# A gated mixer block with a 32-expert layer: the experts' weights fetched as 1 MB pieces into sixteen places instead of 2 MB pieces into eight

## The reference, cut to what matters

```python
h2 = rmsnorm(x, ffn_norm_g)                       # 256 tokens x 1024
logits = h2 @ router_w + router_b                 # 32 experts, the best 4 of each token are used
for e in range(32):
    g = jnp.minimum(t @ w_gate[e] + b_gate[e], 7.0)
    u = jnp.clip(t @ w_up[e] + b_up[e], -7.0, 7.0)
    act = (u + 1.0) * (g * jax.nn.sigmoid(1.702 * g))
    out = out + comb[:, e:e + 1] * (act @ w_down[e] + b_down[e])
```

## Time and profile before

| | before |
|---|---|
| device time, median of 3 runs | 1172.27 us (1169.89 to 1173.79) |
| span of the profiled execution | 1169.7 us |
| PE busy | 1102.9 us (94%) |
| DVE, ACT, POOL busy | 281.6, 190.4, 62.6 us |
| bytes read from HBM | 431.21 MB |
| mean rate over the span | 370 GB/s |
| experts' transfers | 192 of 2048 KB |

### The profile page before, as it was taken

The page is one execution under the profiler, slowest core; times in us unless marked ns, Lnnn a source line. Parts: engine busy times, 40 slices in busy tenths (PEclk is TensorE's granted clock), DMA queues, the critical chain, the costliest instruction groups (busy, mean ns, idle before and its releaser), DMA issues.

```text
span 1169.7 us, 13269 instructions
## 1 busy us (share of the span) xinstructions
PE 1102.9 (94%) x5385; PEld 463.3 (40%) x5385; DVE 281.6 (24%) x632; ACT 190.4 (16%) x361; POOL 62.6 (5%) x58
## 2 busy tenths in 40 slices
PE   6998998999999999999999999999999999999998
PEld 3787995333333333333333333333333333333332
DVE  4978664111111111111111111111111111111112
ACT  3645632100110010001000100001000100010000
POOL 0194120000000000000000000000000000000000
PEclk9989998999999999999999999999999999999999
DMA  8612478799999999999999999999999999999996
GB/s 314 256 73 108 171 295 334 293 402 409 409 409 409 410 409 409 409 410 410 409 409 410 410 409 410 409 410 410 409 409 410 410 410 409 410 410 409 409 409 259
DMA packets 116942, 432.55 MB, mean 370 GB/s; under 512 B 5557, under 2 KB 6106, under 8 KB 116922
## 3 DMA queue, kind: packets, MB, share of 16 engines
q1 hardware_dynamic: 116634, 431.60, 93.3%
q10 hardware_dynamic: 288, 0.67, 0.2%
HBM read 431.21 MB, written 1.05 MB: 370 GB/s over the span
## 4 chain that ended last, share of the span: by engine, by line
PE 48%; DMA 41%; DVE 7%; ACT 2%; SPq 1%; issue 1%; DVEq 0%; ACTq 0%
DMA ring<-in_exp_w_up 41%; PE ps L752 27%; PE ps L711 5%; PE ps L759 3%; PE ps L717 3%; PE ps L724 2%; PE ps L490 2%; PE ps L492 2%; PE ps L491 2%; DVE ring_r L1071 1%; DMA ring<-in_w_in 1%; SPq L434 1%; ACT ring_r L812 1%; DVE arena L1140 1%; DVE arena L1126 1%; PE ps L777 1%
## 5 line engine op out<-in xcount | busy, mean ns | idle before, releaser
L752 PE MATMUL ps<-ring,arena 128*64 128x512 f32 x3072 | 685.9, 594 | 32.5 <-DMA ring<-in_exp_w_gate 28.0
L752 PEld LDWEIGHTS ps<-ring,arena 128*64 128x64 f32 x3072 | 218.9, 137 | 486.8 <-issue 414.5
L1315 DVE TENSOR_SCALAR arena<-ps 128x512 f32<-128x512 f32 x32 | 22.1, 692 | 507.6 <-PE ps L752 507.6
L759 PE MATMUL ps<-arena 128*64 128x512 f32 x384 | 102.9, 614 | 0.3 <-issue 0.3
L1325 DVE TENSOR_SCALAR arena<-ps 128x512 f32<-128x512 f32 x32 | 22.1, 692 | 244.4 <-PE ps L752 244.4
L969 ACT COPY arena<-ps 128x512 f32<-128x512 f32 x32 | 18.8, 587 | 333.9 <-PE ps L711 333.9
L724 PE MATMUL ps<-arena 64*128 64x512 f32 x264 | 65.6, 615 | 0.8 <-ACT arena L975 0.8
L967 ACT ACTIVATE arena<-arena 128x512 f32<-128x512 f32 x32 | 20.1, 630 | 280.7 <-DVE arena L1315 280.7
L490 PE MATMUL ps<-ring_r 128*128 128x256 f32 (+1 forms) x192 | 61.1, 318 | 4.2 <-DVE ring_r L1071 2.4
L711 PE MATMUL ps<-arena 128*64 128x512 f32 x264 | 64.0, 607 | 0.8 <-DVE arena L1261 0.8
L975 ACT COPY arena<-ps 128x512 f32<-128x512 f32 x32 | 18.8, 586 | 249.0 <-PE ps L752 249.0
(11 more groups left out here) (185 smaller groups left out, 637.6 us busy)
## 6 DMA issues: line engine op xcount, KB each, us to landing
ring<-in_exp_w_gate SPq DMA_DIRECT2D x64, 2048.0 KB, 23.5
ring<-in_exp_w_up SPq DMA_DIRECT2D x64, 2048.0 KB, 23.7
ring<-in_exp_w_down SPq DMA_DIRECT2D x64, 2048.0 KB, 23.7
ring<-in_w_in SPq DMA_DIRECT2D x8, 2048.0 KB, 9.4
ring<-in_w_out SPq DMA_DIRECT2D x2, 2048.0 KB, 7.8
xt<-in_x SPq DMA_DIRECT2D x4, 512.0 KB, 6.9
ring<-in_pool_up SPq DMA_DIRECT2D x1, 2048.0 KB, 7.9
ring<-in_attn_up SPq DMA_DIRECT2D x1, 2048.0 KB, 8.6
```

What stands on the lines that cost most here:

```text
L752: last = mm(ps[BLOCK * half:BLOCK * (half + 1), bank, :], src[:, c, k % 2, :], slot(n)[:, c, HALF * half:HALF * (half + 1)], start=False, ...
L759: mm(ps[BLOCK * half:BLOCK * (half + 1), bank, :], this_e[:, buf, k, :], bias_rows[:, HALF * half:HALF * (half + 1)], start=True, stop=False)
L1315: v.tensor_scalar(g1, ps[:, 4, :], LIMIT, None, ALU.min).then_inc(g_ready, 1)
```

## The change: 1 MB pieces, sixteen places, one run of 8 KB per partition

Each place is halved (`PART_W`), which makes sixteen (`RING`), and an expert's weights are twelve pieces, four for each matrix (`PARTS_OF_W`). The rows are dealt to the partitions in another way: row `512 * h + 4 * p + 2 * d + c` goes to partition p. So the two rows of a piece that go to one partition are neighbours in HBM, and lie in it and in SBUF as one run of 8 KB; the next partition's run begins 16 KB further, and the other half of each 16 KB is the next piece.

The products must meet the features in the same order. Where a feature is placed is decided when DVE writes `h2` and `act_out`: both are now written through a permuted pattern (chunk-major in memory, read in the natural order), so that each 32-bit result goes 512 bytes behind the one before. The gains of the norm, which came from a turned tile `cols`, are now loaded in that order by one small transfer of their own on ACT's queue. The number of matrix products and their sizes stay as they are. The front's pieces get semaphores of their own (`front_in`).

```diff
-PIECES_PER_EXPERT = 6
+PIECES_PER_EXPERT = 12
+PARTS_OF_W = PIECES_PER_EXPERT // 3
+RING = 16
+PART_W = PIECE // 2
...
-                        w = A[name][0].rearrange("e (c p) n -> p e c n", p=P)
-                        for half in range(2):
-                            n = PIECES_PER_EXPERT * j + 2 * m + half
-                            if first and n < SLOTS:
-                                front_piece_free(sp, LEFT_BY[n])
+                        w = A[name][0].rearrange("e (h p d c) n -> p e h d (c n)", h=2, p=P, d=2)
+                        for part_w in range(PARTS_OF_W):
+                            n = PIECES_PER_EXPERT * j + PARTS_OF_W * m + part_w
+                            if first and n < RING:
+                                front_piece_free(sp, LEFT_BY[n // 2])
                             else:
...
-                                sp.wait_ge(piece_done, at * (UNROLL * PIECES_PER_EXPERT) + (n - SLOTS + 1))
-                            src = w[:, bass.ds(step * UNROLL + j, 1), 4 * half:4 * half + 4, :]
-                            src = src.rearrange("p e c n -> p (e c) n")
-                            sp.dma_start(slot(n), src).then_inc(slot_in[ORDER[n % SLOTS]], 16)
+                                sp.wait_ge(piece_done, at * (UNROLL * PIECES_PER_EXPERT) + (n - RING + 1))
+                            half, pair_of = divmod(part_w, 2)
+                            src = w[:, bass.ds(step * UNROLL + j, 1), half:half + 1, pair_of:pair_of + 1, :]
+                            src = src.rearrange("p e h d n -> p (e h d n)")
+                            sp.dma_start(slot_flat(n), src).then_inc(slot_in[n % RING], 16)
...
-                        def product(k, bank, src):
-                            n = PIECES_PER_EXPERT * j + k
-                            pe.wait_ge(slot_in[ORDER[n % SLOTS]], landed + 16 * (BEFORE[n % SLOTS] + n // SLOTS + 1))
-                            for c in range(4):
-                                for half in range(2):
-                                    last = mm(ps[BLOCK * half:BLOCK * (half + 1), bank, :], src[:, c, k % 2, :],
...
-                            last.then_inc(piece_done, 1)
+                        def product(m, bank, src):
+                            for k in range(PARTS_OF_W):
+                                n = PIECES_PER_EXPERT * j + PARTS_OF_W * m + k
+                                pe.wait_ge(slot_in[n % RING], landed + 16 * (n // RING + 1))
+                                for c in range(2):
+                                    for half in range(2):
+                                        last = mm(ps[BLOCK * half:BLOCK * (half + 1), bank, :],
+                                                  src[:, 2 * (k % 2) + c, k // 2, :],
...
+                                last.then_inc(piece_done, 1)
...
+            act.dma_start(gain[:], A["ffn_norm_g"].rearrange("l (h p c) -> p (l h) c", h=2, p=P)).then_inc(gain_in, 16)
...
-                    v.tensor_scalar(h2[:, t, part_cols], xt[:, t, part_cols], rstd[:, t:t + 1], None,
+                    v.tensor_scalar(h2[:, t, part_cols].rearrange("q (c p) -> q p c", c=4),
+                                    xt[:, t, part_cols].rearrange("q (p c) -> q p c", c=4), rstd[:, t:t + 1], None,
                                     ALU.mult).then_inc(h2_ready, 1)
...
-                        v.scalar_tensor_tensor(out=act_out, in0=u1, scalar=1.0, in1=gs, op0=ALU.add,
+                        v.scalar_tensor_tensor(out=act_out.rearrange("q (c p) -> q p c", c=4),
+                                               in0=u1.rearrange("q (p c) -> q p c", c=4), scalar=1.0,
+                                               in1=gs.rearrange("q (p c) -> q p c", c=4), op0=ALU.add,
                                                op1=ALU.mult).then_inc(act_ready, 1)
```

More of the change, by code:

```diff
@@ L100, in build @@
         cols = sb("cols", [P, R_ROWS])
+        gain = sb("gain", [P, 2, 4])
         small = sb("small", [P, 256])
@@ L233, in build @@
         PARAMS = len(params)
-        slot_in = [sem(f"slot_in{i}") for i in range(SLOTS)]
+        front_in = [sem(f"front_in{i}") for i in range(4)]
+        slot_in = [sem(f"slot_in{i}") for i in range(RING)]
         piece_done = sem("piece_done")
@@ L241, in build @@
         rows_in = sem("rows_in")
+        gain_in = sem("gain_in")
         par_in = sem("par_in")
@@ L361, in build @@
         assert sorted(ORDER) == list(range(SLOTS))
-        BEFORE = [len([n for n in range(FRONT) if n % LAND == k]) for k in ORDER]
         def as_chunks(ap, wide):
@@ L375, in split_slot, with slot_flat @@
             return tuple(as_chunks(ap, wide) for ap in split_piece(n))
+        def slot_flat(n):
+            k = n % RING
+            return ring[:, ORDER[k // 2], PART_W * (k % 2):PART_W * (k % 2 + 1)]
         def slot(n):
-            return as_chunks(ring[:, ORDER[n % SLOTS], :], True)
+            return slot_flat(n).rearrange("p (c n) -> p c n", c=2)
         h_split = tuple(ring_r[H_SLOT][:, NC * S * i:NC * S * (i + 1)].rearrange("p (c s) -> p c s", c=NC)
@@ L436, in _ @@
                     front_piece_free(sp, n - LAND)
-                sp.dma_start(front_slot(n, wide=src.shape[1] == 4), src).then_inc(slot_in[n % LAND], 16)
+                sp.dma_start(front_slot(n, wide=src.shape[1] == 4), src).then_inc(front_in[n % LAND], 16)
                 if n == GB_P + 1:
@@ L482, in piece_wait @@
             def piece_wait(n):
-                pe.wait_ge(slot_in[n % LAND], 16 * (n // LAND + 1))
+                pe.wait_ge(front_in[n % LAND], 16 * (n // LAND + 1))
             def split_wait(n, q):
@@ L742, in _ @@
                     done = (r * STEPS + step) * UNROLL
-                    landed = (r * STEPS + step) * (16 * UNROLL * PIECES_PER_EXPERT // SLOTS)
+                    landed = (r * STEPS + step) * (16 * UNROLL * PIECES_PER_EXPERT // RING)
                     for j in range(UNROLL):
                         buf = j % 2
-                        def product(k, bank, src):
-                            n = PIECES_PER_EXPERT * j + k
-                            pe.wait_ge(slot_in[ORDER[n % SLOTS]], landed + 16 * (BEFORE[n % SLOTS] + n // SLOTS + 1))
-                            for c in range(4):
-                                for half in range(2):
-                                    last = mm(ps[BLOCK * half:BLOCK * (half + 1), bank, :], src[:, c, k % 2, :],
-                                              slot(n)[:, c, HALF * half:HALF * (half + 1)],
-                                              start=False, stop=(k % 2 == 1 and c == 3))
-                            last.then_inc(piece_done, 1)
+                        def product(m, bank, src):
[6 more added lines that the diff above has]
+                                                  src[:, 2 * (k % 2) + c, k // 2, :],
+                                                  slot(n)[:, c, HALF * half:HALF * (half + 1)],
+                                                  start=False, stop=(k == PARTS_OF_W - 1 and c == 1))
+                                last.then_inc(piece_done, 1)
                         def biases(k, bank):
@@ L764, in _ @@
                         product(0, 4, h_in[:, buf])
-                        product(1, 4, h_in[:, buf])
                         pe.wait_ge(y_ready, done + (j + 1))
@@ L769, in _ @@
                         biases(1, 5)
-                        product(2, 5, h_in[:, buf])
-                        product(3, 5, h_in[:, buf])
+                        product(1, 5, h_in[:, buf])
                         pe.wait_ge(pick_ready, done + (j + 2))
@@ L782, in _ @@
                         biases(2, 7)
-                        product(4, 7, actT)
-                        product(5, 7, actT)
+                        product(2, 7, actT)
             pe.wait_ge(pickT_ready, rounds * E + 1)
@@ L807, in hi_part @@
                 if q == 0:
-                    act.wait_ge(slot_in[n % LAND], 16 * (n // LAND + 1))
+                    act.wait_ge(front_in[n % LAND], 16 * (n // LAND + 1))
                     if k >= HIS:
@@ L973, in _ @@
                         nc.scalar.copy(pickT, ps[:, 5, 0:S]).then_inc(pickT_ready, 1)
-                        act.wait_ge(piece_done, done * PIECES_PER_EXPERT + (PIECES_PER_EXPERT * j + 6))
+                        act.wait_ge(piece_done, done * PIECES_PER_EXPERT + (PIECES_PER_EXPERT * j + PIECES_PER_EXPERT))
                         nc.scalar.copy(y_e, ps[:, 7, :]).then_inc(y_ready, 1)
@@ L1298, in gathered_in @@
             def gathered_in(buf):
-                gain = cols[:, R_FFNG:R_FFNG + NC].rearrange("p (h c) -> p c h", h=2)
                 v.tensor_tensor(h_in[:, buf], ps[:, 6, :].rearrange("p (c h s) -> p c h s", c=4, h=2),
-                                wide(gain, [P, 4, 2, BLOCK], 3), ALU.mult).then_inc(h_in_ready, 1)
+                                wide(gain[:].rearrange("p h c -> p c h"), [P, 4, 2, BLOCK], 3),
+                                ALU.mult).then_inc(h_in_ready, 1)
```

(9 more changed lines are left out.)

## The result

The changed kernel takes 1143.2 us (median, 1140.85 to 1145.84), the kernel before, run beside it, 1172.14. The ratio is 0.9756, with a 95% interval of 0.9737 to 0.9775. The profiled execution took 1143.35 us with a span of 1141.1 us; before the span was 1169.7.

A forecast was written before the change was run, and what follows sets the result against it. Weight transfers at 409.6 GB/s, not PE, set the end. 1172.3 - 23.3 (8 KB runs) - 1.7 (earlier refill) - 1.8 (finer end) + 0.5 (`h2`) + 0.3 (`act_out`) = 1146.3, stated as 1146 us; range 1135 to 1171.

The forecast's parts named there:

- The bound: Whole loop: the rate at which 402.65 MB of weights come in, 409.6 GB/s, sets the end, not PE.
- The packet's fixed part: Weight loads: each packet pays 8.0 ns whatever its size, so 8 KB runs save 23.3 us over 364 pieces.
- the earlier refill: Loop start: PE frees a place after half of the products, so the first refill leaves 1.7 us earlier.
- The cut at 4 KB: Rival on weight packets: hardware cuts runs at 4 KB, only the ends gain, 1169.6 us; 0.17 together with the limit in bytes.
- the limit in bytes: Rival on the transfer rate: 409.6 GB/s is a limit in bytes, 1169.6 us; 0.17 together with the 4 KB cut.
- the small fixed part: Rival on weight packets: the fixed part is only 4.6 or 1.0 ns, giving 1156 or 1167 us; chance 0.16.
- HBM's order: Rival on weight reads: HBM likes taking every other 8 KB less; at 330 ns per packet 1198 us; chance 0.07.
- Twice as many transfers: Weight queue: six more transfers per expert cost 0, at most 1.7 us.
- The finer ends: Loop's two ends: first refill 1.7 us earlier, products behind the last up load 1.8 us shorter; bounds 0 and 3.5 us.
- The queue is not always deep: Weight queue: the prediction said it is always deep, so neither SP nor one transfer's latency sets the rate.
- The permuted writes: VectorE: `act_out` 0.33 us dearer, covered in the loop, 0.3 us in the last expert; `h2` 0.5 us.
- PE's floor: Whole kernel: if PE alone set the time, a span of 1124.6 us, or 1127.2 on the median's scale.

The follow-up runs named there:

- the plain writes: Changed kernel with `h2` and `act_out` written without the permutation: 1140.73 us, ratio 0.9753 to the kernel before.
- the solid stretch: Changed kernel with a piece's 8 KB runs one behind the other, so a transfer reads 1 MB in one stretch: 1139.5 us, ratio 0.9729 to the kernel before.
- Small pieces alone: Changed kernel with the old row order (4 KB runs) and plain writes, keeping twelve 1 MB pieces in sixteen places: 1168.92 us, ratio 0.9969 to the kernel before.

## Why the prediction was right, point by point

**The bound** was right. The transfers set the end before and after; the plain writes, which free PE by 0.23 us per expert, change nothing that can be told in the changed kernel, and a change of the rate alone (4 KB to 8 KB runs in 2 MB pieces) gives nearly all of the gain.

**The packet's fixed part** had the right mechanism and was sized a little low. I took 8.0 ns between four windows that said 1.0 to 9.4. The loop's packets of 8 KB take 310.6 ns, not 312, a fixed part of 9.4 ns. With 364 pieces that is 27.4 us instead of 23.3, 4.1 us more than the sum had, where forecast and measurement differ by 2.8. The longest window, that of `w_in` over 6 us, was the right one; the two that gave 4.6 and 1.0 ns misled. The term that errs the other way is the earlier refill, 1.7 us, below. With both put right the sum is 1146.3 - 4.1 + 1.7 = 1143.9 us, against 1143.2 measured: the two errors cancelled in part, so some of the nearness of the number is luck.

**The cut at 4 KB, the limit in bytes, the small fixed part and HBM's order** are excluded: by the packet count, by 387, 410, 422 and 429 GB/s for 2, 4, 8 and 16 KB, and by the solid stretch with the same 422. The last holds for 8 KB runs 16 KB apart; no run here had them further apart.

**Twice as many transfers** cost nothing that can be seen: 384 pieces of 1 MB and 192 of 2 MB both run at 422 GB/s in runs of 8 KB, and both at 410 in runs of 4 KB. The time of 1 MB in the table of the Trainium skill ("DMA: Bandwidth & Descriptors", section Bandwidth), 6.15 us, is not what a piece costs in a full queue, which is 2.485 us here. The rule of that section, at least 1 MiB in a transfer, is met by both kernels, so these runs don't test it. What gained here was the longer run, not a larger transfer.

**The finer ends** were put at 3.5 us. Small pieces alone give 3.6 us (2.1 to 5.3), and there the end goes as forecast: from the products behind the last load of up it takes 20.0 us (1146.86 to 1166.9) instead of 21.7 (1147.99 to 1169.7). In the changed kernel 1.7 us are seen behind the last load too, but by another route: the last load waited for is in the gate matrix, not in up. The other 1.7 us, the earlier refill, is not found again at the end: the refill did leave 2.0 us earlier, but the 26.9 us by which the last gate load is earlier are already the 180 pieces of 2 MB up to it times 0.150 us, 27.0.

**The queue is not always deep,** though the prediction said so: at the loop's start it runs dry. With the ring full and PE in its first expert, the rate between 205 and 210 us is 9 GB/s before and 3 after. The next places come free at PE's pace, and faster transfers only wait longer for them: 394 and 387 GB/s before, 384 and 381 after, from 220 to 228 and from 228 to 236 us. (That is also why the first stretch shows 408 and 420 GB/s, and not 410 and 422.) Up to 264 us the changed kernel loses in this way about 1.3 us more than the kernel before, an estimate from the bytes moved in windows of 1 us, so most of the head start; where the rest went stays open. The slices, too, were read a little early: the ninth shows 402 GB/s, and 409 begins with the tenth.

**The permuted writes** were estimated at 0.33 us for `act_out` and measured 0.36; for `h2` at 0.21 per instruction, and it was 0.29. Both lie within their bounds, and in the loop the cost was covered, as forecast. That the last expert pays for `act_out`, and the half microsecond at `h2`, can't be told: the loop's first products begin at 206.83 instead of 207.28 us, and the front's variation is larger than the cost.

**PE's floor.** Forecast 1127 us with the old products. With 28.68 us per expert and the loads out of the way (runs of 16 KB) 1133.7 us were measured, 6.5 above the forecast floor; 0.23 x 32 = 7.4 us were to be expected from the longer period. The room between changed kernel and floor was thus half of what I thought, 9.5 us instead of 19.

## What to carry to other kernels

When transfers set the time and the queue is always full, take the slope from the trace: the time of a packet at two run lengths gives the fixed part, and the fixed part times the packets saved on each DMA engine is the gain. Read it in long windows with a deep queue. Lengthen the contiguous run per partition by choosing which row goes to which partition, and look for the cheapest place where the operand can take on the new order; cutting the same bytes into twice as many transfers of 1 MB left the rate as it was, and gained only at the ends. Look at the queue in the loop's first microseconds as well: where places come free at the compute engine's pace, faster transfers gain nothing.

Then look at the engine that stands next: here PE's period per expert was 4% shorter than the loads' (28.68 against 29.82 us), and the edit that serves the transfers lengthens its work, so the next step (16 KB) met it at once.

## What the runs showed of the hardware that I had not expected

The fixed part of a packet is the same over a factor of eight in size. In the loop with a full queue a packet takes 84.7 ns for 2 KB (387 GB/s), 160.0 ns for 4 KB (409.6), 310.6 ns for 8 KB and 611.7 ns for 16 KB (both from the distance of the products behind loads): each is a time for the bytes and 9.3 to 9.4 ns. The bytes' time is worked out from the 4 and 8 KB packets: 310.6 - 160.0 = 150.6 ns for 4 KB more, 27.2 GB/s for each engine. So these two sizes set the line, and it is the 2 and 16 KB packets, which fall on it, that test it.

A 512-element float32 instruction of VectorE with a write that steps 512 bytes takes 1057 ns instead of 693, and with two reads that step 16 bytes 1089 ns; one with a single read that steps 16 bytes takes 680 ns instead of 483. TensorE's load of a 128x128 operand that steps 16 bytes takes 209 ns instead of 140.
